# A third expert slab held outside the ring, expert outputs added straight to x in mid pair, and the gate computed in halves

## The chip, the cores and the metric

One core of a Trainium2 chip. The metric is the device time of one execution in microseconds (us); the median of three runs is given for the kernel before.

## The reference

Two transformer blocks over 256 tokens of width 1024, float32 throughout. The first block has attention over latent and context tokens, then a mixture of 32 experts; the second has retention, a convolutional FFN, an S5 layer and another FFN. The change touches the experts and the first product with `w_ada`:

```
mod  = silu(c) @ w_ada + b_ada                       # 6144 columns; the first 2048 are needed first
logits = xt @ w_router + b_router; top 4 of 32 experts per token, gates = softmax of the 4
hcat = xb @ w_in[e] + b_in[e]                        # 1024 -> 2048, each expert for its own tokens
x_glu = min(hcat[:, :1024], 7); x_lin = clip(hcat[:, 1024:], -7, 7)
act  = x_glu * sigmoid(1.702 * x_glu) * (x_lin + 1)
y    = act @ w_out[e] + b_out[e]                     # 1024 -> 1024
x    = x + gt2 * (sum of gate * y over a token's experts)
```

## The kernel before, in words

All weights stream from HBM in slabs of 2 MB (128 partitions x 4096 floats) into a ring of six slots (`ring`). SyncE (SP) issues the loads in one fixed order and waits before each until PE has done with the slab that held the slot. GpSimd (POOL) issues a few loads to places outside the ring (`load_held`, line 2937, and line 2947).

The experts are taken in 16 pairs, 12 slabs a pair: eight of `w_in` (four row blocks, two experts), four of `w_out`. Slab j of a pair is row block j // 2 of expert j % 2. Pair 0 and 1 are experts 0 to 3; from pair `WIDE_PAIR` on, DVE has sorted the other experts by their number of tokens (`order_experts`, line 2419): the pair at `WIDE_PAIR` is the fullest (96 places) with the emptiest (32), all others have 64 places each. What does not fit goes to single passes after the pairs (`jobs`, under `pe.If(n_jobs > 0)`, line 1486), six slabs each.

PE's order in one pair (`experts`, line 1360), with the work of the other engines:

- wait for the tokens' columns `x_e` (ACT copies them from PSUM), then `up(0)` to `up(3)`: each multiplies `x_e` with two slabs of `w_in`, 32 PE instructions on the trace, into PSUM banks 0 to 3;
- ACT copies each bank to `h_cat` as its last product lands; PE turns the four pieces (`turn_h`, 1402) into banks 6 and 7; DVE adds the bias (2492), clamps (2501, 2504), scales (2505), ACT takes one tanh over all 1024 columns (1919), DVE multiplies twice (2507, 2508), and only the last of these releases `act_ready`;
- `gather` (1345): the next pair's tokens are selected; in the last pair it gathers for a job that may not exist;
- `scatter` (1356): the pair before's outputs `y_slot` times its gates `g_slot`, in four chunks into banks 6 and 7; DVE adds each chunk to `y_moe` (`add_scattered`, 2452 to 2461);
- the gates are transposed (1422), PE waits for `act_ready`, then `down(4)` and `down(5)` with two slabs of `w_out` each. ACT copies the result to `y_slot`.

Two slabs of pair 1 are held outside the ring (`HELD_EXPERT = (3, 7)`): slab 3 in `h_moe` and `sq`, slab 7 in the place of the `decay` constants, in `b_out_sb` and in `rstd`. `early_w` holds slab 2 of pair 0. After the pairs, PE loads `n_jobs` into a register (1485), jumps over the passes (1486), scatters the last pair's output (`last_scatter`); DVE adds eight tiles `y_moe * mod` to `x` and the last chunks (`last_scattered`, 2512), and norm 3 follows.

At the start, SP loads small inputs, `x`, constants, then four slabs of `w_ada`, each 512 columns over all 1024 rows, so its pieces in HBM are 2 KB long (`cols`, 730); the expert slabs come in pieces of 16 KB. PE multiplies each slab with the condition (`modulation_rows`, 1069, matmul at 1079) as it lands.

Of the kernel before, what the change touches and what calls it, by code (L numbers as in the profile page):

```python
# [44 lines left out]
WIDE_PAIR = 2  # L45
# [3 lines left out]
SORTED = E - 2 * WIDE_PAIR  # L49
ALPHA = 1.702  # L50
# [120 lines left out]
SUMMED_1 = 8  # L171

# [163 lines left out]
HELD_EXPERT = (3, 7)  # L336
# [8 lines left out]
def places():  # L345
# [8 lines left out]
    for j in HELD_EXPERT:  # L354
        loads[slot_at(MOE_0 + j)] -= 1
# [35 lines left out]
def transformer_blocks_kernel(nc, small, const, xT, cT, pos, w_ada, w_qkv, w_o, w_router, w_in,  # L391
# [3 lines left out]
    with ctx:  # L395
# [34 lines left out]
        class Carve:  # L430
# [5 lines left out]
            def __call__(self, *shape):  # L436
# [6 lines left out]
                if len(shape) == 3:  # L443
# [18 lines left out]
                    for a in (p_t[:, 0, :], p_t[:, 1, :], flat(ctx_x[:, 0:4, :]), flat(ctx_x[:, 4:8, :]))]  # L462
# [8 lines left out]
        y_moe = cut(KD, T)  # L471
# [4 lines left out]
        tanh_e = cut(KD, P)  # L476
# [23 lines left out]
        pairwise = flat(tanh_e)[:, 0:SORTED * SORTED].rearrange("p (a b) -> p a b", b=SORTED)  # L500
        key_of, rank_of, is_hot = (cum[:, SORTED * n:SORTED * n + SORTED] for n in range(3))
        is_cold, place_of, order_f = (flat(flags)[:, SORTED * n:SORTED * n + SORTED] for n in range(3))
        sums_of = b_out_sb.rearrange("p (k n) -> p k n", n=P)
# [5 lines left out]
        held_expert_w = [[(0, 0, flat(h_moe)), (1, 0, flat(sq))],  # L509
                         [(0, 0, con("decay")), (1, 0, b_out_sb), (1, 1024, flat(rstd))]]  # L510
# [140 lines left out]
        held_in = [sem(f"held_expert_in{n}") for n in range(len(HELD_EXPERT))]  # L651
# [239 lines left out]
        def _(sp):  # L891
# [50 lines left out]
            for j in range(12):  # L942
                if j in HELD_EXPERT:
                    continue
                if j - 6 in HELD_EXPERT:
                    sp.wait_ge(moe.rows_done, 4)
                else:
                    pair_left(1, j)
                load(MOE_0 + j, expert_source(2 + j % 2, j // 2))
            sp.wait_ge(order_ready, 1)  # L950
            with sp.Fori(2, PAIRS) as i:
# [54 lines left out]
        def _(pe):  # L1006
# [62 lines left out]
            def modulation_rows(key):  # L1069
# [5 lines left out]
                w = slab(key)  # L1075
                for k in range(KD):
# [283 lines left out]
            def experts(s, halves, i, full, tile, first=False, wide=False):  # L1360
# [7 lines left out]
                def rows(j, act, k_tiles, n_slabs, banks, j0):  # L1368
# [5 lines left out]
                    if last or halves == 1:  # L1374
                        order.sort(key=lambda t: t[1])
                    for kk, p in order:
                        k = k_tiles * (j - j0) + kk
                        for n, size, e in tiles:
                            at = n if halves == 2 else CAP * (k % 2)
                            w = tile(halves * j + e, k_tiles, kk, BANK * (p - banks[0]))  # L1380
# [7 lines left out]
                def up(j):  # L1388
                    rows(j, x_e, UP_TILES, 4, (0, 1, 2, 3), 0)
# [4 lines left out]
                def turn_h(c):  # L1394

                    pe.wait_ge(s.h_copied, i * 4 + (c + 1))
# [11 lines left out]
                for j in range(4):  # L1408
                    up(j)
# [1751 lines left out]
```

## Time and profile before

| what | value |
|---|---|
| median of 3 runs | 2109.33 us (2108.92 to 2109.97) |
| the profiled execution | 2109.2 us |
| its span, first to last instruction | 2107.4 us |
| mean granted TensorE clock | 0.978 |
| busy: PE, DVE, ACT, POOL | 1965.2, 627.9, 396.2, 186.0 us |
| HBM read | 613.20 MB |

The profiled execution's own time is 1.8 us more than its span and within 0.2 us of the median. Stages on the span's clock: modulation and attention to about 268 us, the 16 pairs from 275.5 to 1206 us, the second block after that.

### The profile page before, as it was taken

The page shows a single profiled execution, that of the slowest core. Times are in us where ns is not written, and L with a number is a line of the kernel's source. Part 1 is how long each engine was busy: PE and PEld are TensorE (multiplying, and loading weights), DVE is VectorE, ACT ScalarE, POOL GpSimd, SP SyncE. Part 2 cuts the span into 40 slices and gives each one's busy share as a digit, 9 for nine tenths or more (in the row PEclk, how much of TensorE's full clock was granted, in tenths as well). Part 3 has the DMA queues.
Part 4 walks back from the last instruction along what each step waited for, and adds up shares of the span by engine and source line. Part 5 has one row for each costly group of instructions (what it writes and reads, how often), then busy time and mean ns, then how long its engine had stood idle before and what let it go on. Part 6 is the DMA issues. An engine that isn't in the chain of part 4 may idle for free.

```text
span 2107.4 us, 24331 instructions
## 1 busy us (share of the span) xinstructions
PE 1965.2 (93%) x9778; PEld 1252.6 (59%) x9778; DVE 627.9 (30%) x1301; ACT 396.2 (19%) x746; POOL 186.0 (9%) x239
## 2 busy tenths in 40 slices
PE   6999999989998998899989899999999999989998
PEld 4645654334444444333444475788888879868887
DVE  2767342112222122111223245332015127210421
ACT  3126211101111101111111121221122133320210
POOL 0000000000000000000000000010936920000000
PEclk9999999999999999999999999999999999989999
DMA  9986689999999999999999976825334343524330
GB/s 359 367 301 240 254 367 397 418 419 425 423 427 425 428 428 429 429 429 428 428 428 423 411 274 241 317 81 180 120 122 146 138 147 129 202 98 160 110 110 20
DMA packets 121707, 615.32 MB, mean 292 GB/s; under 512 B 5184, under 2 KB 9408, under 8 KB 94240
## 3 DMA queue, kind: packets, MB, share of 16 engines
q1 hardware_dynamic: 120304, 606.53, 72.2%
q0 software_dynamic: 1328, 7.73, 1.0%
q8 instruction: 54, 0.88, 0.2%
q14 instruction: 21, 0.17, 0.0%
HBM read 613.20 MB, written 1.05 MB: 291 GB/s over the span
## 4 chain that ended last, share of the span: by engine, by line
PE 72%; DMA 14%; DVE 8%; issue 3%; ACT 3%; SPq 1%; DVEq 0%; ACTq 0%
PE psum L1040 32%; PE psum L1381 23%; DMA ring<-in_w_in_dram 13%; PE psum L1051 3%; PE psum L1356 2%; PE psum L1267 1%; PE psum L1516 1%; PE psum L1140 1%; DVE arena L2492 1%; PE psum L1691 1%; PE psum L1079 1%; DMA ring<-in_w_ada_dram 1%; DVE arena L2507 1%; PE psum L1665 1%; PE psum L1633 1%
## 5 line engine op out<-in xcount | busy, mean ns | idle before, releaser
L1381 PE MATMUL psum<-ring,arena 128*64 128x512 f32 (+1 forms) x3216 | 690.3, 607 | 68.0 <-DMA ring<-in_w_in_dram 67.1
L1040 PE MATMUL psum<-arena,ring 128*128 128x256 f32 (+1 forms) x3072 | 684.1, 385 | 6.1 <-ACT arena L1770 6.1
L1040 PEld LDWEIGHTS psum<-arena,ring 128*128 128x128 f32 x3072 | 585.4, 191 | 102.9 <-issue 22.5
L1381 PEld LDWEIGHTS psum<-ring,arena 128*64 128x64 f32 (+1 forms) x3216 | 236.6, 136 | 504.6 <-issue 504.6
L1903 ACT ACTIVATE arena<-psum 128x512 f32<-128x512 f32 x146 | 83.8, 574 | 784.3 <-PE psum L1381 682.5
L2492 DVE TENSOR_TENSOR arena<-psum,arena 128x512 f32<-128x512 f32 x60 | 38.6, 685 | 372.2 <-PE psum L1402 372.2
L2776 DVE SCALAR_TENSOR_TENSOR consts<-psum,smalls,consts 128x255 f32<-128x255 f32 (+1 forms) x88 | 38.4, 478 | 232.4 <-ACT consts L2043 231.7
L2471 DVE TENSOR_SCALAR arena<-consts,arena 128x64 f32<-128x64 f32 (+2 forms) x64 | 15.7, 310 | 308.5 <-PE psum L1381 308.5
L1356 PE MATMUL psum<-arena 128*128 128x256 f32 (+1 forms) x272 | 67.9, 393 | 13.6 <-DVE arena L2460 10.0
L2956 POOL DMA_DIRECT2D arena<-in_pos_dram x1 | 0.5, 541 | 903.7 <-PE psum L1495 903.7
L1810 ACT ACTIVATE arena<-psum 128x512 f32<-128x512 f32 (+1 forms) x49 | 27.2, 558 | 233.2 <-PE psum L1040 175.6
L1345 PE MATMUL psum<-arena 128*128 128x128 f32 x544 | 66.4, 282 | 0.0
L1356 PEld LDWEIGHTS psum<-arena 128*128 128x128 f32 (+1 forms) x272 | 50.0, 194 | 27.2 <-DVE arena L2460 16.0
L1345 PEld LDWEIGHTS psum<-arena 128*128 128x128 f32 x544 | 64.9, 199 | 0.0
L2335 DVE SCALAR_TENSOR_TENSOR x<-psum,mod,x 128x256 f32<-128x256 f32 x28 | 13.0, 482 | 162.9 <-PE psum L1040 152.3
L1051 PE MATMUL psum<-ring,arena 128*128 128x512 f32 x128 | 55.1, 592 | 0.0
L1733 ACT ACTIVATE sq<-x 128x512 f32<-128x512 f32 x24 | 14.9, 628 | 205.2 <-DVE x L2335 180.7
L2187 DVE SCALAR_TENSOR_TENSOR arena<-ring,cond,arena 128x512 f32<-128x512 f32 x70 | 52.6, 752 | 2.5
L1079 PE MATMUL psum<-ring,cond 128*32 128x512 f32 x352 | 43.1, 620 | 7.1 <-DMA ring<-in_w_ada_dram 7.1
L2043 ACT ACTIVATE consts<-psum,smalls 128x256 f32<-128x256 f32 x44 | 22.4, 561 | 116.1 <-PE psum L1040 116.1
L1402 PE MATMUL psum<-consts,arena 128*128 128x128 f32 x256 | 37.1, 280 | 7.4 <-DVE arena L2492 6.6
L2460 DVE TENSOR_TENSOR arena<-arena,psum 128x512 f32<-128x512 f32 x60 | 39.8, 684 | 12.0 <-PE psum L1356 12.0
(395 smaller groups left out, 1607.7 us busy)
## 6 DMA issues: line engine op xcount, KB each, us to landing
ring<-in_w_in_dram SPq DMA_DIRECT2D x125, 2048.0 KB, 14.8
ring<-in_w_out_dram SPq DMA_DIRECT2D x64, 2048.0 KB, 17.1
ring<-in_w_ada_dram SPq DMA_DIRECT2D x36, 2048.0 KB, 13.3
ring<-in_w_up_dram SPq DMA_DIRECT2D x22, 2048.0 KB, 7.8
ring<-in_w_ret_dram SPq DMA_DIRECT2D x12, 2048.0 KB, 12.7
ring<-in_w_down_dram SPq DMA_DIRECT2D x16, 1408.0 KB, 5.8
ring<-in_w_qkv_dram SPq DMA_DIRECT2D x4, 2048.0 KB, 19.9
ring<-in_w_rout_dram SPq DMA_DIRECT2D x4, 2048.0 KB, 11.3
```

What stands on the lines that cost most here:

```text
L1040: ins = nc.tensor.matmul(bank(c)[:, at:at + n], w[:, k, m * P:m * P + P], r, start=(k == 0), stop=(k == k_tiles - 1))
L1051: ins = nc.tensor.matmul(bank((key, first_chunk + t))[:, 0:width], lhs(k, t), w[:, k, at:at + width], start=(k == 0), stop=(k == KD - 1))
L1079: ins = nc.tensor.matmul(psum[32 * q:32 * q + 32, b, :], at, w[:, k, :], start=(s == 0 and k < 4), stop=(last and k >= 4))
L1345: ins = nc.tensor.matmul(psum[:, c, m * P:m * P + width], h_tok[:, t, k * P:k * P + P], sel[:, t, 0:width], start=(t == 0), stop=(t == TT ...
L1356: ins = nc.tensor.matmul(psum[:, 6 + c % 2, m * T:m * T + T], y[:, k * P:k * P + P], g, start=True, stop=True)
L1381: ins = nc.tensor.matmul(psum[at:at + size, p, :], act[:, k, n:n + size], w, start=(k < 3 - halves), stop=(k >= KD - 3 + halves))
L1402: ins = nc.tensor.transpose(out, of, con("ident"))
L1903: nc.scalar.activation(out, src, ACT.Copy).then_inc(signal, 1)
L2187: ins = V.scalar_tensor_tensor(out=out, in0=w[:, k, :], scalar=c[:, k, :], in1=out, op0=ALU.mult, op1=ALU.add)
L2460: ins = V.tensor_tensor(y, y, scattered, ALU.add)
L2492: V.tensor_tensor(dst.rearrange("p k (e n) -> p k e n", n=CAP), src.rearrange("p k (e n) -> p k e n", n=CAP), bb.unsqueeze(3).to_broadcast ...
L2776: ins = V.scalar_tensor_tensor(out=cv[:, a, lag:T], in0=ps[:, a, 0:T - lag], scalar=w[:, 2 - lag, k:k + 1], in1=cv[:, a, lag:T], op0=ALU.m ...
```

## The change

- The scatter of the pair before moves between `up(1)` and `up(2)`. DVE adds each chunk, times `mod`, straight to `x` (eight additions of 128x256 a pair in place of four of 128x512); `y_moe` goes, and with it the eight additions of `last_scattered`.
- The pieces of `h` are produced, copied and turned in the order 0, 2, 1, 3 (`TURNS`), so that the first half of glu and lin is there first; clamp, tanh and gate run on halves of 512 columns, and `down(4)` waits for the first half alone, `down(5)` for the second. tanh is written over `h_cat`, so `tanh_e` goes.
- Three slabs are held in place of two: (pair 1, slab 3), (pair 2, slab 3) and (pair 2, slab 7). The new one lies where `y_moe` (`held_a`, 1 MB) and `tanh_e` (`held_b`, 0.5 MB) were and in 0.5 MB at the arena's end (`held_c`). POOL issues `held_a` right behind `early_w`, the other 1 MB once bank ("cols", 5) is read, and the rest of the third slab after the first scatter.
- `WIDE_PAIR` goes from 2 to 3, as pair 2 must be known beforehand.
- The last pair leaves the loop: no gather in it, and `n_jobs` is loaded before it; the passes gather for themselves. DVE's list of jobs is made before the loop of pairs.
- The first four slabs of `w_ada` become 256 rows of 2048 columns each (pieces of 8 KB); each slab then feeds four column groups with 8 products, as many as before.

```diff
-WIDE_PAIR = 2
+WIDE_PAIR = 3
+TURNS = (0, 2, 1, 3)
+FIRST_ROWS = 4
-HELD_EXPERT = (3, 7)
+HELD_SLABS = ((1, 3), (2, 3), (2, 7))
...
+            if kind == "ada" and s < FIRST_ROWS:
+                return w_ada[T * s:T * s + T, 0:4 * BANK].rearrange("(k p) n -> p k n", p=P)
...
+                if group == 0:
+                    for n in range(2):
+                        k = 2 * s + n
+                        for c in range(4):
+                            ins = nc.tensor.matmul(psum[32 * c:32 * c + 32, b, :], cond32[:, k, 6 - 2 * c:38 - 2 * c],
+                                                   w[:, n, BANK * c:BANK * c + BANK], start=(k == 0), stop=(k == KD - 1))
...
+                if halves == 1:
+                    gather(s, 1, i + 1)
                 pe.wait_ge(s.x_copied, i * 2 + 2)
-                for j in range(4):
+                for j in range(2):
                     up(j)
-                for c in range(4):
-                    turn_h(c)
-                gather(s, halves, i + 2)
...
                     pe.wait_ge(s.y_copied, i * 2)
-                    scatter(s, 4, i * 4 + 3, y_slot, g_slot)
+                    scatter(s, 0, i * 4 + 1, y_slot, g_slot)
+                for j in range(2, 4):
+                    up(j)
+                for n, c in enumerate(TURNS):
+                    turn_h(n, c)
+                if halves == 2 and not last:
+                    gather(s, 2, i + 2)
...
-                pe.wait_ge(s.act_ready, i + 1)
+                pe.wait_ge(s.act_ready, i * 2 + 1)
                 down(4)
+                pe.wait_ge(s.act_ready, i * 2 + 2)
...
-            with pe.Fori(WIDE_PAIR + 1, PAIRS) as i:
+            with pe.Fori(WIDE_PAIR + 1, PAIRS - 1) as i:
                 experts(moe, 2, i, loop_full(i), tile_in_ring)
             pe.wait_ge(over_ready, 1)
             n_jobs = pe.value_load(...)
+            experts(moe, 2, PAIRS - 1, loop_full(PAIRS - 1), tile_in_ring, last=True)
...
+                    for m in range(2):
+                        k = 2 * c + m
+                        ins = V.scalar_tensor_tensor(out=x[:, k, :], in0=psum[:, 6 + c % 2, m * T:m * T + T],
+                                                     scalar=mod[:, 40 + k, 0:1], in1=x[:, k, :], ...)
...
+                turned(0)
+                turned(1)
+                limited(0)
+                turned(2)
+                turned(3)
+                gated(0)
+                limited(1)
+                gated(1)
...
             read_ready(pool, ("ob", 3))
             pool.dma_start(flat(early_w), up_tiles(0, 2)).then_inc(early_in, 16)
+            load_held(1, held_w[1][:1])
...
             read_ready(pool, ("htok", 3))
-            load_held(0, held_expert_w[0])
-            pool.wait_ge(moe.x_ready, 8)
-            load_held(1, held_expert_w[1][1:])
+            load_held(0, held_w[0])
+            read_ready(pool, ("cols", 5))
+            load_held(1, held_w[1][1:])
+            pool.wait_ge(moe.x_ready, 4)
+            load_held(2, held_w[2][1:])
```

`turned(n)` is the bias addition of one piece, `limited(n)` the clamps and scaling of one half, `gated(n)` its two products after tanh.

## Rows read from the trace of the kernel before

**Rows 1.** Stretches: us, busy per engine (instructions), clock, DMA share, GB/s

```profile
8.00:29.00 21.00, 12.53 (x64) 6.03 (x64) 4.12 (x8) 2.12 (x3) 0.00 (x0) 0.90 1.05 387
...
205.00:240.00 35.00, 32.38 (x162) 23.53 (x154) 13.58 (x30) 7.94 (x18) 0.53 (x1) 0.95 0.31 113
...
268.00:290.00 22.00, 21.27 (x102) 12.50 (x103) 8.52 (x27) 2.48 (x3) 0.00 (x0) 0.86 0.70 282
...
320.00:330.00 10.00, 10.00 (x48) 3.32 (x46) 0.00 (x0) 2.48 (x3) 0.00 (x0) 1.00 0.85 292
...
395.00:1180.00 785.00, 703.71 (x3540) 308.14 (x3542) 155.53 (x317) 98.81 (x146) 0.00 (x0) 0.98 1.01 427
...
1300.00:2107.00 807.00, 780.01 (x3885) 665.96 (x3884) 226.31 (x449) 174.58 (x361) 179.83 (x225) 0.98 0.40 144
```

**Rows 2.** Waits of PE, whole run: total us, times, longest

```profile
PE psum L1381 <- DMA ring<-in_w_in_dram: 67.1, 41, 2.9
...
PE psum L1079 <- DMA ring<-in_w_ada_dram: 7.1, 3, 3.5
```

**Rows 3.** PE's timeline, opening: start, us, instructions [idle before <-releaser]

```profile
18.19 1.92 PE L1079 MATMUL psum<-ring,cond 128*32 128x512 f32 x16 [0.68 <-DMA ring<-in_w_ada_dram]
23.61 2.48 PE L1079 MATMUL psum<-ring,cond 128*32 128x512 f32 x16 [3.50 <-DMA ring<-in_w_ada_dram]
29.03 3.21 PE L1079 MATMUL psum<-ring,cond 128*32 128x512 f32 x16 [2.95 <-DMA ring<-in_w_ada_dram]
```

**Rows 4.** PE's timeline, turns of `h` in pairs 0 and 1

```profile
303.11 1.09 PE L1402 MATMUL psum<-consts,arena 128*128 128x128 f32 x8
...
355.45 1.09 PE L1402 MATMUL psum<-consts,arena 128*128 128x128 f32 x8
```

**Rows 5.** Timeline of all engines, last pair

```profile
1154.90 7.09 PE L1381 MATMUL psum<-ring,arena 128*64 128x512 f32 x32 [0.68 <-DMA ring<-in_w_in_dram]
...
1164.69 8.78 PE L1381 MATMUL psum<-ring,arena 128*64 128x512 f32 x32 [2.71 <-DMA ring<-in_w_in_dram]
...
1174.48 7.09 PE L1381 MATMUL psum<-ring,arena 128*64 128x512 f32 x32 [1.00 <-DMA ring<-in_w_in_dram]
...
1181.50 1.09 PE L1402 MATMUL psum<-consts,arena 128*128 128x128 f32 x8
...
1182.19 1.29 DVE L2492 TENSOR_TENSOR arena<-psum,arena 128x512 f32<-128x512 f32 x2 [25.45 <-PE psum L1402]
...
1183.60 0.69 DVE L2501 TENSOR_SCALAR arena<-arena 128x1024 f32<-128x1024 f32 x1
...
1184.09 3.74 PE L1345 MATMUL psum<-arena 128*128 128x128 f32 x32
...
1184.32 1.06 ACT L1919 ACTIVATE arena<-arena 128x1024 f32<-128x1024 f32 x1 [2.12 <-DVE arena L2501]
...
1187.06 1.22 DVE L2507 SCALAR_TENSOR_TENSOR arena<-arena 128x1024 f32<-128x1024 f32 x1
...
1187.67 1.89 PE L1356 MATMUL psum<-arena 128*128 128x256 f32 x8
...
1192.34 13.95 PE L1381 MATMUL psum<-ring,arena 128*64 128x512 f32 x64
```

**Rows 6.** Timeline, after the last pair: PE's last scatter, DVE's additions

```profile
1209.42 5.69 PE L1356 MATMUL psum<-arena 128*128 128x256 f32 x16 [3.13 <-issue]
...
1213.05 0.88 DVE L2523 SCALAR_TENSOR_TENSOR x<-psum,mod,x 128x256 f32<-128x256 f32 x2 [0.64 <-PE psum L1356]
```

**Rows 7.** Stretch around the last scatter, columns as in rows 1

```profile
1209.00:1213.00 4.00, 3.58 (x9) 2.93 (x10) 0.88 (x2) 0.41 (x1) 0.00 (x0) 0.57 1.06 388
```

**Rows 8.** PE's sequencer at lines 1485 and 1486

```profile
L1485 PEldq TENSOR_LOAD <-arena x1: 491/491/491, 1202.1 to 1202.1; - x1
L1486 PEldq COMPARE_BRANCH  x1: 6225/6225/6225, 1203.0 to 1203.0; - x1
```

**Rows 9.** Page, part 6: slab loads of `w_in`

```profile
ring<-in_w_in_dram SPq DMA_DIRECT2D x125, 2048.0 KB, 14.8
```

More of the change, by code:

```diff
@@ L940, in pair_left @@
                     sp.wait_ge(moe.rows_done, i * 4 + (j // 2 - 2))
[L942 to L949, printed above, removed]
+            for i in range(1, WIDE_PAIR):
+                for j in range(12):
+                    if (i, j) in HELD_SLABS:
+                        continue
+                    if (i, j - 6) in HELD_SLABS:
+                        sp.wait_ge(moe.rows_done, i * 4)
+                    else:
+                        pair_left(i, j)
+                    load(MOE_0 + j, expert_source(2 * i + j % 2, j // 2))
             sp.wait_ge(order_ready, 1)
-            with sp.Fori(2, PAIRS) as i:
+            with sp.Fori(WIDE_PAIR, PAIRS) as i:
                 of_pair = [sp.value_load(order[0:1, bass.ds(i * 2 + h, 1)], min_val=0, max_val=E - 1) for h in range(2)]
@@ L1358, in scatter, with experts @@
                     ins.then_inc(s.x_ready, 1)
-            def experts(s, halves, i, full, tile, first=False, wide=False):
+            def experts(s, halves, i, full, tile, first=False, wide=False, last=False):
                 width = CAP * halves
@@ L1374, in rows @@
                     if last or halves == 1:
-                        order.sort(key=lambda t: t[1])
+                        order.sort(key=lambda t: banks.index(t[1]))
                     for kk, p in order:
@@ new lines, in pair_full, with full, pair_tile, tile @@
+            def pair_full(i):
+                def full(j):
+                    if (i, j) in HELD_SLABS:
+                        n = HELD_SLABS.index((i, j))
+                        pe.wait_ge(held_in[n], 16 * len(held_w[n]))
+                    else:
+                        held = [h for h in HELD_SLABS if h < (i, j)]
+                        pe.wait_ge(ring_full[slot_at(MOE_0 + j)], 32 * i + 16 * loads_of(j, held))
+                return full
+            def pair_tile(i):
+                def tile(j, k_tiles, kk, n0):
+                    if (i, j) not in HELD_SLABS:
+                        return tile_in_ring(j, k_tiles, kk, n0)
+                    for tile_k, at, w in held_w[HELD_SLABS.index((i, j))]:
+                        if tile_k == kk and at <= n0 < at + w.shape[1]:
+                            return w[:, n0 - at:n0 - at + BANK]
+                return tile
@@ L1932, in _ @@
             n_jobs = act.value_load(jobs[0:1, MAX_JOBS + 2:MAX_JOBS + 3], min_val=0, max_val=MAX_JOBS)
+            experts(moe, 2, PAIRS - 1, last=True)
             with act.If(n_jobs > 0):
@@ L2569, in _ @@
             dve.wait_ge(over_ready, 1)
+            with dve.Fori(WIDE_PAIR + 1, PAIRS - 1) as i:
+                experts(moe, 2, i, pair_at(i), 0, pair_at(i + 1))
             def job_at(i):
```

168 lines of the change are left out of this document (83 added, 85 removed).

## The prediction

> **What bounds the kernel now.** I read the stretches first [rows 1]. The 16 pairs of experts take 44% of the time, and from 395 to 1180 us the DMA engines are never free: share 1.01 at 427 GB/s. PE is busy for 704 of those 785 us. The waits of PE [rows 2] say the same from the other side: 67.1 us in 41 waits of `up` for slabs of `w_in`, more than for anything else. One slab (2.097 MB) takes 4.91 us at 427 GB/s, so a pair's 12 take 58.9. Ahead of that stretch the queue is partly free: 113 GB/s from 205 to 240 us, 282 from 268 to 290, 292 from 320 to 330. So the pairs end when the last slab has come plus what PE does behind it, and a slab moved into the free time moves that end. In the second block (from 1300 us) PE is busy 780 of 807 us and DMA is 0.40 full; the change does not touch it, and it should only shift.
>
> The opening is bound by DMA too. PE waits for each slab of `w_ada`, and they come 5.42 us apart [rows 3], which is 2.097 MB at the 387 GB/s of the first stretch.
>
> While PE sets the pace, a pair takes 52.3 us (from 303.11 to 355.45) [rows 4]. That is 6.6 less than its slabs take. In the last pair [rows 5] the `up`s start 9.79 us apart, two slabs each, and `up(3)` at 1174.48. Then comes what no slab delays: turns from 1181.50, gather 3.6, scatter with the gate transposes 4.7, `down` from 1192.34, 13.95 long. The last scatter starts 3.13 us after that, with idle time for which the trace names no releaser [rows 6].
>
> **Part A, rows of `w_ada`.** Four slabs come in pieces of 8 KB in place of 2 KB. The trace has 387 GB/s with 2 KB pieces and 427 with 16 KB; 8 KB is not shown at full load. I take 427 for being nearer to 16 KB in length: 4.91 in place of 5.42 a slab. PE starts on the fourth at 29.03 after four such transfers: 4 x 0.5 = 2.0, less 0.2 as 8 KB is shorter than 16: **-1.8**. The fourth slab's products took 3.21 us against 1.92, at the lower clock, and may do so again. Bounds: 0 (rate unchanged) to -2.5 (it also escapes part of the low clock). The count of products is the same. Behind it PE works to the experts without waiting for a slab, so the shift carries through attention.
>
> The Trainium skill (DMA: Bandwidth & Descriptors, Specifications) gives 512 B as the least transfer for line rate; by that the 2 KB pieces are at full rate already and A would be 0. The two rates of rows 1 speak against it; it is rival 1.
>
> **Part B, a third slab held.** SP's queue has one slab less, in pair 2, where the queue is full: -4.9 on every later arrival. POOL's gets 2 MB more. Half of it (`held_a`) is issued right behind `early_w` in the 35 us at 113 GB/s, of which (1 - 113/427) x 35 = 25.7 us are free; it takes 2.5. The other half is issued once bank ("cols", 5) is read, at about 268 us, into 22 us of which 7.5 are free; it takes 2.5. Behind it on POOL stand only the rest of the third slab and, far later, `pos`. That rest (1 MB) now goes at the end of the first scatter, about 294 us in place of 314, and is needed a pair later than today: nothing. SP's new waits (slab 9 of pairs 1 and 2 for `down(4)` of the pair before) stand in line behind later ones, and slab 7 of pair 1, now in the ring, waits for `up(0)` only. PE gains 6.6 us a pair on the queue until it waits for it, so it catches up one pair later than now, in pair 3. **-4.9**. Bounds: -2.5 (only `held_a` finds free time) to -6.5 (the mid-pair scatter also fills part of the 3.2 us free at 320 to 330).
>
> **Part C, the order in a pair.** In a pair bound by DMA the moved scatter costs nothing until it delays `up(3)`. In the last pair: `up(1)` from 1154.90 to 1162.0, scatter 4.4, `up(2)` from 1166.4 to 1173.5, still before the slabs of 1174.48. Its cover there is 1.0 us; if it takes 5.4, `up(3)` starts late by the rest. DVE now does two additions of 128x256 a chunk, 0.88 us together [rows 6], where one addition of 128x512 from PSUM takes 0.65 [rows 5]; PE's four products take 0.95, so in two banks the pace stays PE's. It was DVE's turn products that held the scatter until now; in mid pair DVE is idle. The eight additions of `last_scattered` ran under `down` and save nothing.
>
> Behind `up(3)` of the last pair: gather and scatter go, and what is late next is the half activation. DVE from 1182.19: two bias additions to 1183.5, three operations on 512 columns (half of 0.69, with gaps: 1.2) to 1184.8, two bias additions to 1186.1 (tanh of a half, half of 1.06, is done by 1184.7, also behind a table load), two products of half 1.22 with gaps: 1187.5. `down(4)` starts at 1187.6 in place of 1192.34: **-4.8** (-4 to -5, by the gaps between the halves). The second half needs 2.9 us more of DVE and is done by 1190.5, under `down(4)`. In loop pairs the gather (3.6) stays and covers this chain with 0.5 us to spare, and were it uncovered the slack of the DMA would take it.
>
> This leaves PE idle for about 2.9 us before `down(4)`. After the 3.13 us of idle time at 1206 to 1209 the clock was granted at 0.57 over 4 us, at 1.2 in place of 2.4 GHz for most of them [rows 7]: 4 x 0.43 = 1.7 us lost. I expect the same here: **+1.7** (0 to 1.7; above it nothing, as the products then run on without idle time).
>
> **Part D, the end of the last pair.** The jump over the passes takes 6.2 us on PE's sequencer, begun at 1202.95 when the last products were still running, and behind 0.9 us of loading and testing `n_jobs` [rows 8]. The load now comes before the last pair, in its 4.4 us of waits for slabs: **-0.9** (0, if the jump is held by something else, to -1.0). The jump itself stays. ACT's and DVE's loads move likewise; both are idle there.
>
> **At nothing:** the wide pair one later; sorting 26 experts for 28; the list of jobs (a dozen small operations on DVE) between pairs 3 and 4, where DVE is idle 80% of the time, and were it not covered, PE's slack of 6.6 us a pair would take it; the scatter in pairs 0 to 2, which PE bounds: as long as today's 4.4, bound +3 (three pairs at +1).
>
> **Sum.** -1.8 - 4.9 - 4.8 + 1.7 - 0.9 = -10.7 against the profiled 2109.2 (0.13 below the median): **2098.5 us**. The bounds together give -15 and -2; not all fall on one side.
>
> **Rivals.**
> 1. Pieces of 2 KB are at full rate, A is 0: PE goes on waiting at 5.4 us steps, 2100.3. For it: both stretches have a full DMA share. Against: at the same share they moved 387 and 427. 0.10.
> 2. The held slab only fills the queue earlier and the ring stalls later: between `down` of a pair and `up(2)` of the next PE now frees slots later by the scatter, the free time at 320 to 330 us grows and more like it appears, and B gives 1 or less: 2102.5. For it: in the first three pairs PE bounds, and the queue waits for it. Against: 2.5 us lie where nothing else is asked for, 25.7 us wide. 0.14.
> 3. More: fewer stalls of the ring, no lowered clock before `down(4)`: B -6.5, +1.7 gone, 2095.2. 0.10.
> 4. Slower: the mid-pair scatter makes PE the bound of every pair. It stands between products now, and if PE's chunks and DVE's do not overlap (PE 0.95, DVE 0.88, two signals) it takes 8 us, which adds 3.6 and stays below 6.6. It decides from 11 us on. At 12 us a pair takes 59.9, 1.0 over the slabs; over 15 pairs +15, and B is lost: about 2118. For it: the last scatter, with the same operations, took 5.69 [rows 6]. Against: half of that ran at the lower clock, and it is far from 11. 0.03.
> 5. It does not do what it says: an expert 4 or 5, now outside the sorting, has over 64 tokens, and a single pass of six slabs (29 us) follows: 2128. Today 125 loads and three outside the ring make 128 = 32 x 4 slabs, so no pass runs [rows 9]. Counted from the reference's inputs, the fullest expert is 7 with 66 and expert 4 has 60. 0.01.
>
> **Chances.** The forecast 0.62, the rivals as above. Range 2093 to 2105: it takes in rivals 1 to 3 and the bounds of B, C and D one at a time, and leaves out rivals 4 and 5 and the case of several bad bounds together. About 0.2% (4.2 us) is what a measurement can tell from no change: faster 0.88, same 0.08, slower 0.04.
>
> **What would show it.** The fourth `w_ada` slab's products at 27.2 in place of 29.03. PE's first wait for a slab of `w_in` in pair 3, not 2. 427 GB/s in the pairs as before, `up(3)` of the last pair at 1167.8. From its end to `down(4)` 6.1 us in place of 10.8, with a wait for DVE, and the clock lowered behind it. The last scatter 2.2 us after the last product. Wrong would be: mid-pair scatters over 5.4 us with `up(3)` late behind them, or new stretches below 420 GB/s after 400 us.

## The result and the profile after

| | before | after |
|---|---|---|
| median (runs) | 2109.12 us (4; 2107.42 to 2109.97) | 2090.55 us (4; 2088.70 to 2093.88) |
| profiled execution, span | 2109.2, 2107.4 | 2091.67, 2089.9 |
| busy PE, DVE | 1965.2, 627.9 | 1959.6, 641.8 |

The ratio of after to before is 0.9915, with a 95% interval of 0.9898 to 0.9932. The time fell by 18.6 us where 10.7 were forecast, and lies below the range.

The stretches of the kernel after (us, busy per engine, granted clock, DMA share, GB/s; to be read beside [rows 1]):

```profile
8.00:29.00 21.00, 15.24 (x76) 6.67 (x80) 4.12 (x8) 2.10 (x3) 0.00 (x0) 0.82 1.01 416
205.00:240.00 35.00, 32.37 (x154) 23.88 (x152) 12.93 (x28) 7.41 (x16) 1.05 (x2) 0.95 0.43 159
268.00:290.00 22.00, 21.16 (x102) 11.66 (x102) 8.66 (x29) 2.48 (x3) 0.00 (x0) 0.94 0.90 362
290.00:320.00 30.00, 29.56 (x153) 13.13 (x153) 8.79 (x18) 4.91 (x9) 1.05 (x2) 0.94 0.96 394
320.00:330.00 10.00, 10.00 (x50) 3.40 (x48) 0.00 (x0) 2.48 (x3) 0.00 (x0) 1.00 0.88 313
370.00:380.00 10.00, 8.78 (x42) 2.81 (x40) 0.00 (x0) 1.97 (x3) 0.00 (x0) 1.00 1.01 429
395.00:1165.00 770.00, 698.44 (x3592) 292.56 (x3592) 173.00 (x438) 94.64 (x155) 0.00 (x0) 0.98 1.01 428
```

The first row has 416 GB/s for 387. From 205 to 240 and from 268 to 290 us the queue carries 46 and 80 GB/s more than before: 1.6 and 1.8 MB, the held slab and part of what follows. In the pairs the rate is what it was, 428. The waits of PE for `w_in` still stand first (total, times, longest):

```profile
PE psum L1401 <- DMA ring<-in_w_in_dram: 65.6, 32, 2.7
...
PE psum L1401 <- DVE arena L2561: 2.7, 1, 2.7
```

The opening, PE's timeline, beside [rows 3]:

```profile
22.24 3.64 PE L1092 MATMUL psum<-ring,cond 128*32 128x512 f32 x16 [3.05 <-DMA ring<-in_w_ada_dram]
27.23 3.64 PE L1092 MATMUL psum<-ring,cond 128*32 128x512 f32 x16 [1.35 <-DMA ring<-in_w_ada_dram]
```

The slabs come 4.99 us apart in place of 5.42, and the fourth's products begin at 27.23 as forecast (27.2). The products of the third and the fourth slab took 3.64 us each where the same 16 take 1.92 at the full clock [rows 3], so nearly all of them ran at 1.2 GHz, and less reached the router's product, which begins at 254.92 in place of 256.04.

The last pair, timeline of PE, ACT and DVE, beside [rows 5, 6]:

```profile
1152.07 1.99 PE L1376 MATMUL psum<-arena 128*128 128x256 f32 x8
1154.25 1.99 PE L1376 MATMUL psum<-arena 128*128 128x256 f32 x8 [0.19 <-DVE x L2495]
1156.18 7.09 PE L1401 MATMUL psum<-ring,arena 128*64 128x512 f32 x32
...
1164.62 7.09 PE L1401 MATMUL psum<-ring,arena 128*64 128x512 f32 x32 [1.35 <-DMA ring<-in_w_in_dram]
...
1171.64 1.09 PE L1422 MATMUL psum<-consts,arena 128*128 128x128 f32 x8
1172.33 1.29 DVE L2538 TENSOR_TENSOR arena<-psum,arena 128x512 f32<-128x512 f32 x2 [15.17 <-PE psum L1422]
...
1173.99 0.63 ACT L1955 ACTIVATE arena<-arena 128x512 f32<-128x512 f32 x1 [1.65 <-DVE arena L2551]
...
1174.67 1.28 DVE L2538 TENSOR_TENSOR arena<-psum,arena 128x512 f32<-128x512 f32 x2
1175.87 0.68 DVE L2560 SCALAR_TENSOR_TENSOR arena<-arena 128x512 f32<-128x512 f32 x1
1176.58 0.69 DVE L2561 TENSOR_TENSOR arena<-arena 128x512 f32<-128x512 f32 x1
...
1177.33 15.65 PE L1401 MATMUL psum<-ring,arena 128*64 128x512 f32 x64 [2.72 <-DVE arena L2561]
...
1195.07 5.47 PE L1376 MATMUL psum<-arena 128*128 128x256 f32 x16 [2.09 <-issue]
...
1200.38 1.89 PE L1527 MATMUL psum<-sq,arena 128*128 128x256 f32 x8
```

`up(3)` begins at 1164.62, where 1167.8 was forecast. PE's first wait for a slab of `w_in` is still in pair 2 (1.22 us at 379.78), not in pair 3 as forecast, and from pair 4 on it waits at `up(0)` and `up(1)` of every pair. The scatter now stands between two `up`s and takes 4.1 us with a wait of 0.19. From the first turn to `down(4)` it is 5.69 us in place of 10.84. `down(4)` and `down(5)` take 15.65 in place of 13.95, and the clock in that place is the one of [rows 7]:

```profile
1178.00:1182.00 4.00, 4.00 (x12) 1.12 (x10) 1.70 (x3) 0.55 (x2) 0.00 (x0) 0.57 0.97 400
```

The last scatter begins 2.09 us after the last product in place of 3.13. The jump stands in it as before (PE's sequencer at line 1518 of the kernel after):

```profile
L1518 PEldq COMPARE_BRANCH  x1: 6277/6277/6277, 1188.5 to 1188.5; - x1
```

**Where the 17.5 us of the two spans are.** Four marks divide them: the router's product (the last long one before the experts), the first turn of the last pair, norm 3 (first product of the second block), and the end.

| stretch | before | after | difference | forecast |
|---|---|---|---|---|
| start to the router's product | 256.04 | 254.92 | -1.12 | -1.8 |
| to the first turn of pair 15 | 925.46 | 916.72 | -8.74 | -4.9 |
| to norm 3 | 33.44 | 28.74 | -4.70 | -4.0 |
| norm 3 to the end | 892.46 | 889.52 | -2.94 | 0 |

Two stretches hold what was missed: the way to the last pair gave 3.8 us more, and the second block, in which no instruction differs, 2.9. The turns show the first. In the kernel after they stand 58.73 us apart from pair 4 (525.64) to pair 15 (1171.64). Before, with as many slabs at nearly the same rate, it is 648.34 us over the same 11 steps (533.16 to 1181.50), and 11 x 58.73 is 646.03: 2.3 us are lost in the loop, 1.7 of them in its last two steps. There the kernel before has one dip:

```profile
1136.00:1140.00 4.00, 4.00 (x22) 1.40 (x20) 3.93 (x4) 0.00 (x0) 0.00 (x0) 1.00 0.99 422
1140.00:1144.00 4.00, 4.00 (x22) 1.32 (x20) 0.01 (x1) 0.04 (x1) 0.00 (x0) 1.00 0.99 360
1144.00:1148.00 4.00, 4.00 (x20) 1.28 (x18) 0.00 (x0) 1.16 (x2) 0.00 (x0) 1.00 0.97 414
```

At 1140.7 `down(4)` had ended and SP issued the next slabs; at 360 GB/s for 4 us the queue brought 0.27 MB less than at 428, 0.6 us of slabs. Its DMA share shows nothing of it. One such row alone proves little: from 672 to 676 us the rate was 389, and no slab was late. What tells is when single slabs land. The slab issued at 1123.36 took 19.9 us and the next one, issued at 1140.69, took 9.2 (SP's timeline, then the DMA view of the two issues):

```profile
1140.69 0.85 SPq L899 DMA_DIRECT2D ring<-in_w_in_dram  x2
```

```profile
ring<-in_w_in_dram SPq DMA_DIRECT2D x1, 2048.0 KB, 19.9
...
ring<-in_w_in_dram SPq DMA_DIRECT2D x1, 2048.0 KB, 9.2
```

So it was issued only 2.5 us before the queue had brought the last slab it held, and landed 6.64 us behind that one, where slabs of a full queue land 4.89 us apart: 1.7 us late. The same place of the kernel after, behind its `down(4)`:

```profile
1126.00:1130.00 4.00, 4.00 (x22) 1.34 (x20) 0.00 (x0) 0.02 (x1) 0.00 (x0) 1.00 1.00 426
1130.00:1134.00 4.00, 3.36 (x16) 0.86 (x12) 0.00 (x0) 1.17 (x2) 0.00 (x0) 1.00 1.00 426
```

### The profile page after: what moved, and what is told of

It is laid out like the page before. It is cut to its first block, busy times and chain, and to the rows that moved or that the text cites. A ratio compares the mean times of both kernels' runs of the same rounds, so it can differ in the third digit from the quotient of the medians.

```text
span 2089.9 us, 24290 instructions
## 1 busy us (share of the span) xinstructions
PE 1959.6 (94%) x9746; PEld 1230.0 (59%) x9746; DVE 641.8 (31%) x1433; ACT 392.2 (19%) x759; POOL 187.9 (9%) x242
## 3 DMA queue, kind: packets, MB, share of 16 engines
HBM read 613.20 MB, written 1.05 MB: 294 GB/s over the span
## 4 chain that ended last, share of the span: by engine, by line
PE 70%; DMA 22%; DVE 4%; ACT 3%; issue 1%; SPq 1%; DVEq 0%; ACTq 0%
PE psum L1052 32%; DMA ring<-in_w_in_dram 21%; PE psum L1401 19%; PE psum L1063 3%; PE psum L1365 1%; PE psum L1376 1%; PE psum L1287 1%; PE psum L1548 1%; PE psum L1160 1%; PE psum L1723 1%; DMA ring<-in_w_ada_dram 1%; PE psum L1099 1%; PE psum L1697 1%; PE psum L1422 1%; PE psum L1665 1%
## 5 line engine op out<-in xcount | busy, mean ns | idle before, releaser
L1401 PEld LDWEIGHTS psum<-ring,arena 128*64 128x64 f32 (+1 forms) x3200 | 223.0, 136 | 508.9 <-issue 436.8
L1935 ACT ACTIVATE arena<-psum 128x512 f32<-128x512 f32 (+1 forms) x144 | 79.0, 571 | 735.2 <-PE psum L1401 729.6
L2495 DVE SCALAR_TENSOR_TENSOR x<-psum,mod,x 128x256 f32<-128x256 f32 x128 | 55.6, 479 | 145.1 <-PE psum L1376 145.1
L1842 ACT ACTIVATE arena<-psum 128x512 f32<-128x512 f32 (+1 forms) x49 | 27.3, 558 | 231.0 <-PE psum L1052 175.9
L2372 DVE SCALAR_TENSOR_TENSOR x<-psum,mod,x 128x256 f32<-128x256 f32 x28 | 13.0, 482 | 162.9 <-PE psum L1052 152.3
L1365 PE MATMUL psum<-arena 128*128 128x128 f32 x512 | 61.5, 280 | 0.0
L1365 PEld LDWEIGHTS psum<-arena 128*128 128x128 f32 x512 | 60.1, 196 | 0.0
L1422 PEld LDWEIGHTS psum<-consts,arena 128*128 128x128 f32 x256 | 27.1, 140 | 26.6 <-issue 20.2
```

The lines of the kernel that those rows point to most:

```text
L1365: ins = nc.tensor.matmul(psum[:, c, m * P:m * P + width], h_tok[:, t, k * P:k * P + P], sel[:, t, 0:width], start=(t == 0), stop=(t == TT ...
L1401: ins = nc.tensor.matmul(psum[at:at + size, p, :], act[:, k, n:n + size], w, start=(k < 3 - halves), stop=(k >= KD - 3 + halves))
L1422: ins = nc.tensor.transpose(out, of, con("ident"))
L1842: read_done(nc.scalar.activation(out, src, ACT.Copy, scale=scale), key)
L1935: nc.scalar.activation(out, src, ACT.Copy).then_inc(signal, 1)
L2495: ins = V.scalar_tensor_tensor(out=x[:, k, :], in0=psum[:, 6 + c % 2, m * T:m * T + T], scalar=mod[:, 40 + k, 0:1], in1=x[:, k, :], op0=AL ...
```

## The experiments

From here "router to last turn" is the second stretch of the table; it leaves out what the opening did by chance. The times of these runs come with a kernel before that was run beside them (medians 2107.42 to 2109.46), so the ratios are to be compared, and the stretches are from one profile each.

### The columns of `w_ada` again

```diff
-FIRST_ROWS = 4
+FIRST_ROWS = 0
```

> The changed kernel with the first four w_ada slabs loaded as columns again (pieces of 2 KB). The changed kernel's fourth slab was used at 27.23 us where it was 29.03 before, but by 248 us PE was only 1.2 us ahead. Theory (each slab came 0.5 us sooner, the lower clock took a third back): products of the slabs again 5.4 us apart, attention 1.2 us later, whole kernel 1.2 us slower than the changed one, about 0.8% faster than before. Rival (the gain of the opening is made or lost by where the clock falls): 0 or 2 us, with the slabs' spacing as before all the same.

2095.54 us (6 runs), 0.9930 of before (0.9910 to 0.9951). The slabs come at 5.42 us steps again and the fourth's products begin at 28.85. The router's product begins at 256.96; router to last turn is 916.83, as with the rows (916.72). So part A is a shift of the whole. The expectation had the whole kernel 1.2 us slower than the changed one; the ratios give about 3 (0.9930 for 0.9915), but their intervals overlap. Its size by the profiles: 255.4, 256.0 and 257.0 for the router's product in the three kernels with 2 KB pieces, 253.0 to 256.4 in the eleven with 8 KB, with 254.5 in their middle: about 1.5 us.

### The third slab through the ring

```diff
-HELD_SLABS = ((1, 3), (2, 3), (2, 7))
+HELD_SLABS = ((1, 3), (2, 7))
```

> The changed kernel with two slabs held, not three (the one of pair 2, row block 1, second expert, goes through the ring). Theory 1 (the held slab is worth its own transfer, the rest of the gain in the pairs comes from the order of the work): up(3) of the last pair starts 4.9 us later than in the changed kernel (1169.5 in place of 1164.6), and the pairs from 4 on stay at 58.7 us each. Theory 2 (the held slab is worth all of the 8.5 us that the pairs gained beyond the opening): 7 to 8.5 us later, or pairs longer than 58.7 again.

2097.69 us (6 runs), 0.9948 (0.9929 to 0.9968). Router to last turn 921.56: the slab is worth 4.84 us, the 4.9 of the forecast. Four other profiles with three slabs and the same code in these pairs have 916.2 to 916.8, which gives 4.7 to 5.4. One expectation failed: the pairs from 4 on did not stay at 58.7. From pair 4 to 15 they take 647.62 us, 1.6 more than in the kernel after, in two steps of 59.93 and 59.13, although `down(4)` starts 6.48 us behind the turn as there. The section on the slots takes this up.

### The scatter back to the end of the pair

The third slab, the halves and the addition to `x` stay.

```diff
-                    scatter(s, 0, i * 4 + 1, y_slot, g_slot)
-                for j in range(2, 4):
+                for j in range(2, 4):
...
+                    scatter(s, 4, i * 4 + 3, y_slot, g_slot)
```

> The changed kernel with the scatter back behind the gather in every pair (still added to x, still halves, still three held). Theory 1 (before, down(4) ended hardly before the queue ran out, so each spell of the lower clock cost queue time; the moved scatter gives 4.4 us of room): the pairs from 4 to 15 take 2 to 3 us more in sum than 12 x 58.7, in steps of up to 1.7 us where the clock fell; up(3) of the last pair 2 to 4 us later; and from there to down(4) 11 us in place of 5.7, without the lowered clock, so in all 6 to 8 us slower than the changed kernel. Theory 2 (the order gives the pairs nothing): pairs at 58.7 us, only the tail is longer, 3.6 to 4 us slower.

2109.11 us (10 runs, 2100.03 to 2121.73), 1.0006 (0.9985 to 1.0027): the whole gain is gone, where 6 to 8 us were expected. The profile is of a run of 2104.92 us, so some 4 us of the median stand in no trace. Router to last turn is 924.39, 7.7 us over the kernel after and only 1.1 below the kernel before. With the scatter late, the held slab and the halves together bring 1.1 us of the 8.7. From pair 4 to 15, 648.58 us: 2.6 more than 11 x 58.73. In the last pair the chain of gate and scatter (PE's timeline) is longer than the one it replaced:

```profile
1180.60 1.23 PE L1422 MATMUL psum<-consts,arena 128*128 128x128 f32 x8 [0.51 <-DVE arena L2537]
1182.92 1.97 PE L1376 MATMUL psum<-arena 128*128 128x256 f32 x8 [1.10 <-DVE arena L2537]
1188.00 3.49 PE L1376 MATMUL psum<-arena 128*128 128x256 f32 x8 [3.12 <-DVE x L2495]
1191.33 0.38 PE L1446 MATMUL psum<-consts,arena 128*128 128x128 f32 x2
1191.64 13.95 PE L1401 MATMUL psum<-ring,arena 128*64 128x512 f32 x64
```

DVE has the activation and the additions to do in one place, and the scatter's second half waits 3.12 us for it: 12.65 from turn to `down(4)`.

### The scatter alone, in the kernel before

```diff
-                for j in range(4):
+                for j in range(2):
                     up(j)
...
+                    scatter(s, 0, i * 4 + 1, y_slot, g_slot)
+                for j in range(2, 4):
+                    up(j)
```

> The kernel before with nothing changed but the place of the scatter and of DVE's four additions to y_moe, in mid pair. Theory 1 (the order alone keeps the queue full): the steps of 0.6 to 1.8 us in the pairs from 3 on go, turn to turn 58.7 us throughout and 2.4 us less from pair 4 to 15; up(3) of the last pair 2 to 5 us earlier than at 1174.5; from the turns to down(4) 8.0 in place of 10.8 us, of which the lowered clock takes 1.7 back. In all 4 to 6 us faster than before. Theory 2 (the order gives the pairs nothing, the held slab gave all): up(3) at 1174.5, steps as before, 1 us faster.

2103.7 us (10 runs), 0.9987 (0.9977 to 0.9996). From pair 4 to 15 it takes 646.02 us: nothing is lost, by the order alone. Router to last turn 924.14, so 1.3 us; the first pairs give 1.0 back. There PE sets the pace and `down(4)` now waits 1.6 us for the whole activation: the second turn comes 53.43 us after the first in place of 52.34. Beside its own kernel before it is 3.7 us faster where 4 to 6 were expected; `up(3)` of the last pair is 2.0 us earlier, and `down(4)` comes 8.10 us behind the turn, as expected, but the clock stayed up behind it (13.95).

### The activation whole

`down(4)` waits for both halves.

```diff
-                pe.wait_ge(s.act_ready, i * 2 + 1)
+                pe.wait_ge(s.act_ready, i * 2 + 2)
                 down(4)
```

> The changed kernel, but down(4) waits for both halves of the activation. In the last pair down(4) starts 2.9 to 3.3 us later behind up(3) (about 8.7 in place of 5.7 us). In the loop down(4) starts about 2.2 us later. Theory 1: of the 4.4 us of room 2.2 are left, still over the 1.7 us of a spell of lower clock, so the pairs stay at 58.7 us, and the first four pairs, bound by PE, pass on up to 2 us: 3 to 5 us slower than the changed kernel. Theory 2: 3 us slower, all of it in the last pair.

2098.20 us (6 runs), 0.9948 (0.9931 to 0.9965). Turn to `down(4)` is 8.15 in place of 5.69. Router to last turn is 919.53, 2.8 us more: in the first pairs the turns stand 53.68 us apart for 52.0 and 53.46. The tail is 31.96 us for 28.74, which makes 6.0 us where 3 to 5 were expected. The gather covers the chain of the first half, as forecast (in the kernel after no pair of the loop waits for DVE there); of the whole chain 1.6 us stay open, and in the first pairs that is lost for good.

### The kernel after once more, and 12 products to keep the clock

Ahead of the last pair's `down(4)`; nobody reads them.

```diff
+                if last:
+                    for n in range(12):
+                        nc.tensor.matmul(psum[:, 0, 0:P], con("ident"), con("ident"), start=True, stop=True)
                 pe.wait_ge(s.act_ready, i * 2 + 1)
```

> The changed kernel once more, on the chip of this call. If the gain beyond the forecast in the second block (3.0 us, where no instruction differs) is chance of the clock, its length here differs from 889.5 us by 1 us or more and falls into what the others show (889.4 to 892.6); if the change makes it, it is 889.5 again. The ratio to before comes nearer to what the traces give without that block: 14.5 us, 0.993.

> The changed kernel with 12 products of 128x128 on constants (2.7 us, a result nobody reads) in the last pair where PE waits for the first half of the activation. If the idle time is what lowers the clock: down(4) starts as before at 5.7 us behind the turns and down(4) and down(5) take 13.95 in place of 15.65, 1.7 us faster. If the clock falls for another reason: 15.65 again.

The kernel after: 2091.00 us (5 runs), 0.9923 (0.9909 to 0.9936). With the products: 2090.36 (5 runs), 0.9918 (0.9904 to 0.9931). PE's timeline with them, and the stretch that stood at 0.57:

```profile
1173.32 2.84 PE L1450 MATMUL psum<-consts 128*128 128x128 f32 x24
1176.20 14.02 PE L1401 MATMUL psum<-ring,arena 128*64 128x512 f32 x64
1192.28 4.37 PE L1376 MATMUL psum<-arena 128*128 128x256 f32 x16 [2.06 <-issue]
1196.48 0.81 PE L1530 MATMUL psum<-sq,arena 128*128 128x256 f32 x3
```

```profile
1177.00:1181.00 4.00, 4.00 (x22) 1.31 (x20) 1.57 (x3) 0.41 (x2) 0.00 (x0) 1.00 1.02 424
```

The products fill the idle time, the clock stays at 2.4 GHz, and `down` takes 14.02. The clock is not lowered at the last scatter either. First turn to norm 3 is 25.97 us in place of 28.94 in the run beside it: 3.0 less, 1.6 of them in `down`. The rest is in the last scatter (4.20 us in place of 5.55), which took 4.20 in three profiles without these products too, so it may be chance. The total doesn't show the gain (0.6 us less): in that profile the second block took 892.3 and in the other 889.2. This is one profile, and in one without the products the clock stayed up as well (16 in mid pair, below: 13.97). That the idle time lowers the clock is likely by this, not proved.

The second block of the kernel after took 889.20 us this time, so the expectation that it would differ from 889.5 by 1 us or more failed: by this test alone the 3 us could belong to the change. But the same instructions of that block took 892.3 with the 12 products, and 892.5 with the columns.

### The load of `n_jobs` behind the last pair

```diff
-            n_jobs = pe.value_load(...)
             experts(moe, 2, PAIRS - 1, loop_full(PAIRS - 1), tile_in_ring, last=True)
+            n_jobs = pe.value_load(...)
```

> The changed kernel with PE's load of n_jobs behind the last pair. Forecast's part D: the last scatter starts 3.0 to 3.1 us behind the last product in place of 2.09, 0.9 to 1.0 slower. Rival (the jump is held by something else): 2.1 again.

2089.26 us in one run. The load and the jump on PE's sequencer, and the scatter after it:

```profile
L1517 PEldq TENSOR_LOAD <-arena x1: 485/485/485, 1186.6 to 1186.6; - x1
```

```profile
L1518 PEldq COMPARE_BRANCH  x1: 6227/6227/6227, 1187.5 to 1187.5; - x1
```

```profile
1194.01 4.37 PE L1376 MATMUL psum<-arena 128*128 128x256 f32 x16 [2.97 <-issue]
1198.21 2.11 PE L1527 MATMUL psum<-sq,arena 128*128 128x256 f32 x9
```

The scatter begins 0.9 us later after the last product than with it ahead of the pair (2.97 to 2.09). But here the clock was not lowered in it (4.20 us to norm 3, where it was 5.31 and 5.55), so the end came no later.

### How long PE may free no slot

Between `up(3)` and the end of `down(4)` PE frees no slot of the ring. In a pair of the loop the first turn and `down(4)` lie 6.48 us apart in the kernel after, 8.10 with the scatter alone moved, 8.15 with the activation whole, 10.84 before and 11.08 with the late scatter. The last two lose time, the first three don't. (The kernel with two slabs held has 6.48 as well, and 1.6 us more in its steps; see below.) So the length of this stretch was varied by itself, with products that nobody reads, in pairs 4 to 14 (here 16):

```diff
                 ins.then_inc(s.gates_turned, 1)
+                for n in range(16):
+                    nc.tensor.matmul(psum[:, 3, 0:P], con("ident"), con("ident"), start=True, stop=True)
```

and as a counter-test the same 16 between the scatter and `up(2)`.

> The kernel after, with 8 products of 128x128 that nobody reads put in front of the wait for `down(4)` in pairs 4 to 14. 12 of them took 2.84 us in the last pair, so these take 1.9, and from the first turn to `down(4)` it is 8.4 us in place of 6.5. Theory 1 (the queue runs thin when PE frees no slot for too long between `up(3)` and `down(4)`; 8.15 and 8.10 us lost nothing, 10.84 and 11.08 lost 2.4 and 2.6): nothing is lost, the turns stay 58.73 us apart from pair 4 to 15. Theory 2 (it is the order alone, any scatter between `up(1)` and `up(2)` cures it): nothing lost either. Theory 3 (it is how much PE has to do in a pair): 0 to 1 us lost.

> The same with 16 products: 3.8 us, 10.3 us from the first turn to `down(4)`, PE's own work in a pair 56 us at the full clock, below the 58.73 of the slabs. Theory 1: 1 to 3 us lost from pair 4 to 15 (steps over 58.8), the time 1 to 3 us over the kernel after. Theory 2: nothing lost. Theory 3: 1 to 3 us lost here and as much with the 16 products in mid pair.

> The same 16 products (3.8 us) put in mid pair, behind the scatter and ahead of `up(2)`, in pairs 4 to 14: PE has as much to do as with them ahead of `down(4)`, but from the first turn to `down(4)` it stays 6.5 us. Theory 1: nothing lost, the turns stay 58.73 us apart. Theory 2: nothing. Theory 3: as much lost as with the products ahead of `down(4)`, 1 to 3 us.

> The 16 unread products ahead of `down(4)` in pairs 4 to 14 made 20: 4.7 us, 11.0 us from the first turn to `down(4)`, which is more than in the kernel before (10.84) and as much as with the scatter back at the end (11.08), where 2.4 and 2.6 us were lost between pairs 4 and 15. With 16 (10.05 us) the loss was 0.16. If the length of that stretch is what counts, with its edge between 10.05 and 10.84 us: 1.5 us or more lost from pair 4 to 15. If it is the order (no other work between `up(1)` and `up(2)`): 0.5 us or less, as with 16.

| kernel | turn to `down(4)` | pairs 4 to 15 | lost | time, runs |
|---|---|---|---|---|
| 8 ahead of `down(4)` | 8.27 | 646.43 | 0.4 | 2094.09 (1) |
| 16 ahead of `down(4)` | 10.05 | 646.19 | 0.2 | 2094.01 (4), 0.9928 |
| 20 ahead of `down(4)` | 10.94 | 647.80 | 1.8 | 2093.54 (7), 0.9920 |
| 16 in mid pair | 6.48 | 643.06 | none | 2090.94 (4), 0.9925 |

The loss is the sum over 11 steps less 646.03. The kernel after and its neighbours have 0 to 0.4 there, from the first step; only the one with two slabs held has 1.6. With 16 the expectation (1 to 3 us) was wrong; with 20 it held, and the losses lie in two steps (59.44 and 59.66 us), as before in few of them. The edge is between 10.05 and 10.94 us, and it is not sharp: beyond it most steps lose nothing. The kernel before stood on it with 10.84: it lost nothing in most pairs, and most in the one where `up(3)` fell on the lowered clock and took 8.60 us in place of 7.09 (PE's timeline, pair 14 of the kernel before):

```profile
1114.03 8.60 PE L1381 MATMUL psum<-ring,arena 128*64 128x512 f32 x32 [2.70 <-DMA ring<-in_w_in_dram]
```

That it is PE's whole work in a pair is out: with the 16 in mid pair nothing is lost. (Its sum is below 646.03 because its turn of pair 4 came 2 us late by the products, of which the last pair has none. Its landing times, below, say the same without a sum. Router to last turn is 914.91, the shortest of all; 1.5 us of that lie ahead of its first turn, where the gather took 3.82 us in place of 5.45, at a higher clock.) One reading is open: 20 also leave PE the least slack, and no counter-test with 20 in mid pair was run.

The landing times of the slabs show the loss where it arises. Call lead the time by which a slab is issued before the one ahead of it lands: while it is long, the queue always has a slab to bring. Call late what the slab lands beyond 4.89 us behind the one ahead. From the turn of pair 4 to the last `up(3)`:

| kernel | shortest lead | late at a lead of 4.1 us or less | late at a lead of 8 us or more |
|---|---|---|---|
| before | 2.55 | 0.55, 1.74 | none |
| scatter late | 3.86 | 0.43, 0.10 | 0.92, 0.93 |
| 20 ahead of `down(4)` | 3.99 | 0.71, 0.95, 0.11 | none |
| 16 ahead of `down(4)` | 4.87 | none | 0.31 |
| 16 in mid pair | 4.95 | none | 0.15 |
| 8 ahead of `down(4)` | 6.67 | none | 0.52 |
| activation whole | 6.79 | none | none |
| scatter alone moved | 6.81 | none | none |
| two slabs held | 8.43 | none | 1.22, 0.28 |
| after | 8.45 | none | none |

In the kernel after run again, with the 12 products and with the late load of `n_jobs`, whose code in these pairs is the same, one slab is late by 0.34 to 0.54 us at a lead of 9.3 to 9.4.

The third column is what the length of the stretch costs: the 2.3 us of the kernel before, and the 1.8 us of the 20 products. With leads of 4.87 us and more nothing is lost that way; with leads of 4.0 to 4.1 a slab is late only now and then. The last column is something else, for the queue was well filled. Each of those slabs lands 2.2 to 6.3 us after a 16 KB transfer of the instruction queue has begun, as here in the kernel with two slabs held, from 534 to 539 us:

```profile
q8 instruction: 1, 0.02, 1.3%
```

That these transfers are the cause is not shown: others like them, in the kernel after at 531.9 and 1139.7, made no slab late. The kernel before and the one with the scatter alone moved have none between 484 and 1190 us. So of the 2.6 us of the late scatter only 0.5 come from its long stretch, and the 1.6 of the kernel with two slabs held don't speak against the edge.

In the first pairs, from the turn of pair 1 to that of pair 4, it is the same: slabs are late by 1.20 and 1.64 us at leads of 2.7 and 3.3 before, by 2.95 at 1.4 with the scatter alone moved, by 0.89 and 2.07 at 3.9 and 2.2 with the activation whole, and by 0.14 in the kernel after. There PE sets the pace, and a longer path through the pair frees the slots later.

## Why the prediction was right in direction and too small

**Part A** held in kind: 416 GB/s and a fourth slab at 27.23. The 1.8 us became about 1.5, since the products behind fell on the lower clock for longer. The profile shows rival 1, the rule of the Trainium skill (DMA: Bandwidth & Descriptors, Specifications) that 512 B are enough for line rate, to be wrong for this stream: 387 with 2 KB, 416 with 8, 428 with 16, at DMA shares of 1.05, 1.01 and 1.01. In the kernel after the slabs stood 5.42 us apart as columns and 4.99 as rows, 8% less.

**Part B, the held slab,** is 4.84 us against 4.9. But it was shown only with the two other parts. The chain from router to last turn goes 925.46 (before), 924.14 (scatter in mid pair), 921.56 (all of the change but the third slab, so halves, addition to `x` and the last pair by itself too), 916.72 (and the slab); everything with the scatter late gives 924.39. So in the old order something like rival 2, that the slab only moves the stall, seems to happen: with the scatter late, slabs of the first pairs are late by 1.16 and 1.47 us at leads of 3.3 and 3.6. The third slab alone in the kernel before was not run, and that it would bring 1 us or less there is argued.

**The step that failed is the first sentence of part C:** "In a pair bound by DMA the moved scatter costs nothing until it delays `up(3)`." I asked there what the move costs and not what it gives, and the sum has nothing for the order and the halves ahead of the last pair. I took a DMA share of 1.01 for a queue that is full, and charged the parts of a pair only where PE waits. The order of the pair decides when slots come free. Before, slabs issued too late landed late by 2.3 us in the loop and by 2.8 in the first pairs, 5.1 in all; in the kernel after that is 0.14. Some of it is lost again to slabs that are late beside code transfers (0.88 us at 508.70, just ahead of pair 4's turn). What is left is 3.9 us that the sum has not: 1.32 by the scatter alone, and 2.58 that come with the rest, for the most part the halves (without them 2.8 are lost). The clause "were it uncovered the slack of the DMA would take it" fails in the first pairs: with the activation whole, the first of them is 1.7 us longer, and the queue ran short behind it. That the gather covers the chain of the first half held. Rival 3 had the direction, with 1.6 us for it and a chance of 0.10.

**The tail** was forecast at -4.0 and is -4.7. Turn to `down(4)` -5.15 (forecast -4.8): DVE's chain had 0.3 us less of gaps than I put in. The lowered clock +1.70 (+1.7), at the place named. The end of the pair -1.25 (-0.9): 1.04 in the idle time, the rest in the scatter's own, which is chance. With `n_jobs` loaded behind the pair the idle time was 2.97 us, so the 0.9 us of part D is shown by a run of its own.

**Rival 4** was far off: 4.1 us for the mid-pair scatter. Its cover was not used up in the last pair, where `up(3)` still waited 1.35 us. In six pairs of the loop (5, 8, 9, 10, 13 and 14) `up(1)` ran at the lower clock (8.5 to 8.8 us) and the wait was 0 to 0.14, so there the cover just sufficed, and the turns stayed 58.73 us apart. DVE's additions, 479 ns each by the page of the profile, ran beside PE's products. **Rival 5** did not happen: 124 slabs of `w_in` through the ring and four outside it make the 128.

**The second block** gave 2.9 us that no part of the change accounts for. In the fourteen profiles it takes 889.2 to 892.5 us, whatever the kernel. The kernel before is at the upper end (892.46), the one after at the lower. In the five profiles with 889.2 to 889.5 the clock is lowered in three places of the block, in the nine with 890.3 to 892.5 in four. The fourth lies 582 to 585 us behind norm 3, here before (first row) and at the same work after:

```profile
1798.00:1806.00 8.00, 6.68 (x23) 5.57 (x24) 5.80 (x17) 6.72 (x15) 0.00 (x0) 0.79 0.99 364
...
1783.00:1791.00 8.00, 7.88 (x37) 6.96 (x38) 5.85 (x19) 6.86 (x16) 0.00 (x0) 1.00 0.81 299
```

So the length goes with the clock; no run changed the clock alone, and why the fourth place comes and goes is open. The change gets no credit for these 2.9 us. The tail is also part chance: the last scatter up to norm 3 took 4.2 or 5.2 to 5.6 us by the clock. Of the profiles' 17.5 us, 14.6 lie ahead of norm 3. The range gave the second block no spread at all. Without those 2.9 us the time would have been 2093.5, just inside the range: that it fell outside is partly chance, but the 3.9 us of part C were missing in any case.

## What to carry to other kernels

A stream at full DMA share is not a stream that can't be helped: compare the distance of equal steps over the whole loop, and where some are longer, look at when single slabs are issued and land, just behind the longest time in which the consumer frees no slot. A load that is issued when the one ahead has only a few us to go is the sign (here 4 us or less, of the 4.89 that a slab takes). Spread the work that frees nothing over the pair before adding memory ahead of it; here the held slab was worth 4.8 us with the order changed, and slab, halves and all the rest 1.1 us from router to last turn with the scatter left late. And ask of a step that moves off a covered place what it gives as well as what it costs.

## What the runs showed that was not expected

- The rate of the same engines at a share over 1 depends on the pieces: 387, 416 and 428 GB/s for 2, 8 and 16 KB.
- The jump over the passes takes PE's sequencer 6.2 to 6.3 us wherever the load of its value stands (6225, 6277, 6227 ns), and 2.1 us of it are open behind the last products. The Trainium skill (Advanced Engine Details and Errata, Control Flow Timing) gives about 108 ns for a compare and branch; the 6.2 us here are far from it, and this jump goes over a long stretch of code. In the traces looked at a 16 KB transfer of the instruction queue begins 3.6 to 3.8 us after the jump (at 1206.65 before, at 1192.30 after), takes 1.1 us, and the jump ends about 1.4 us behind it. That it waits for code fits this; it was not tested.
- The idle time of PE ahead of the last `down(4)` (2.72 us, more with the activation whole) was followed by a lowered clock in nine of the ten profiles whose last pair has no gather, no late scatter and no 12 products; 2.84 us of products that nobody reads, in the same place, left it at 1.00 in the one profile that has them. After 2.1 us of idle time before the last scatter both happened.
- Executions of the kernel after differ by 5 us (2088.70 to 2093.88), those of the kernel before by 7 to 19 in the later sets and those with the late scatter by 22, which is as much as the largest single part of this change is worth or more; parts were told apart by marks inside the trace and not by totals.
